# A hybrid streaming-encoder block on one core: longer warm-up, reordered first tiles and v normalisation, lag kernels in four partition groups, "down" by tokens with x1 added on TensorE

## The reference

```python
h = _rms(x, g_mix)
za, zu, zv, zq, zg = split(h @ w_in)          # 512, 512, 512, 512, 3*1024 columns
ya = gelu(_s5(za, ...))                       # diagonal state space, 32 groups of 16
ya = (ya * sigmoid(ya @ w_glu + b_glu)) @ w_a_out
yb = _sgu(zu, zv, g_sgu, beta_sgu, w_s, b_s) @ w_b_out
       # gelu(zu) * (causal mix over blocks of 128 tokens of layernorm(gelu(zv)) + b_s)
yc = _mem_xattn(zq, mem, g_mem, w_kv) @ w_c_out    # 4 heads of 128, softmax over 256
gates = sigmoid(zg + b_gate)
merged = gates[0] * ya + gates[1] * yb + gates[2] * yc
x = x + merged @ w_out                        # called x1 below
hf = _rms(x, g_ffn)
x = x + (silu(hf @ w_gate) * (hf @ w_up)) @ w_down   # x2; inner width 2816
return _rms(x, g_final)
```

## Time and profile before

| | us |
|---|---|
| median of 3 runs | 813.68 (812.5 to 813.94) |
| the profiled execution, its own time | 813.09 |
| its span, first to last instruction | 811.4 |
| PE busy | 790.8 (97%) |
| DVE busy | 413.4 (51%) |
| ACT busy | 356.6 (44%) |
| POOL busy | 354.1 (44%) |
| moved by DMA | 83.9 MB, 103 GB/s |

### The profile page before, as it was taken

How to read it: one execution, slowest core, us unless ns; L and a number is a source line. 1 busy time by engine, 2 the same in 40 slices (tenths; PEclk the granted TensorE clock), 3 DMA queues, 4 the chain that set the end, 5 groups by cost and what they waited for, 6 DMA issues and landing times.

```text
span 811.4 us, 10169 instructions
## 1 busy us (share of the span) xinstructions
PE 790.8 (97%) x3690; PEld 655.9 (81%) x3690; DVE 413.4 (51%) x625; ACT 356.6 (44%) x520; POOL 354.1 (44%) x182
## 2 busy tenths in 40 slices
PE   7999799999999999999999999999999999999996
PEld 6788687688888888888788788888888888888885
DVE  5899969856566665246765533333333333000035
ACT  5796355633535333634434444444433443122133
POOL 2556646234242434444344344444444444443452
PEclk8999899999999999999999999999999999999997
DMA  7743323022221343232323223322332233233313
GB/s 240 288 153 105 129 72 108 29 79 86 71 91 65 100 160 105 78 102 80 104 83 99 102 82 102 103 97 84 103 103 86 95 103 101 85 100 103 99 57 104
DMA packets 24814, 83.90 MB, mean 103 GB/s; under 512 B 2640, under 2 KB 4816, under 8 KB 24400
## 3 DMA queue, kind: packets, MB, share of 16 engines
q1 hardware_dynamic: 24784, 83.50, 31.0%
HBM read 81.39 MB, written 2.10 MB: 103 GB/s over the span
## 4 chain that ended last, share of the span: by engine, by line
PE 84%; DVE 9%; issue 3%; POOL 2%; DMA 1%; ACT 1%; SPq 0%; POOLq 0%; DVEq 0%; ACTq 0%
PE bank L1305 26%; PE bank L1307 26%; PE bank L1306 26%; DVE pow_tmp L803 2%; POOL w_lo L383 1%; PE bank L1514 1%; PE bank L1399 1%; PE bank L1524 1%; PE bank L1416 1%; DMA raw<-w_dram 1%; DVE vtok L969 1%; DVE mf L1175 1%; DVE bpow L803 1%; DVE tab_tmp L803 1%; DVE cpow L803 1%
## 5 line engine op out<-in xcount | busy, mean ns | idle before, releaser
L383 POOL TENSOR_TENSOR w_lo<-raw,w_hi 128x1024 fp32r<-128x1024 f32 x111 | 268.1, 2416 | 368.1 <-ACT w_hi L460 368.1
L460 ACT ACTIVATE w_hi<-raw 128x1024 fp32r<-128x1024 f32 x133 | 141.0, 1060 | 363.4 <-PE bank L1307 353.6
L1305 PE MATMUL bank<-h_hi,w_hi 128*128 128x512 f32 x640 | 252.6, 395 | 4.9 <-DVE h_lo L808 2.2
L1306 PE MATMUL bank<-h_lo,w_hi 128*128 128x512 f32 x640 | 250.3, 391 | 0.0
L1307 PE MATMUL bank<-h_hi,w_lo 128*128 128x512 f32 x640 | 250.2, 391 | 0.0
L1305 PEld LDWEIGHTS bank<-h_hi,w_hi 128*128 128x128 f32 x640 | 120.7, 189 | 32.7 <-issue 4.4
L1307 PEld LDWEIGHTS bank<-h_hi,w_lo 128*128 128x128 f32 x640 | 120.8, 189 | 25.4
L1306 PEld LDWEIGHTS bank<-h_lo,w_hi 128*128 128x128 f32 x640 | 120.7, 189 | 25.1 <-issue 0.5
L388 POOL TENSOR_TENSOR w_lo<-raw,w_hi 128x512 fp32r<-128x512 f32 x48 | 73.6, 1553 | 60.1 <-ACT w_hi L460 51.1
L1305 PE MATMUL bank<-act_hi,w_hi 128*128 (+2 forms) x176 | 67.0, 381 | 0.0
L1307 PE MATMUL bank<-act_hi,w_lo 128*128 (+2 forms) x176 | 66.8, 379 | 0.0
(11 more groups left out here) (248 smaller groups left out, 1128.9 us busy)
## 6 DMA issues: line engine op xcount, KB each, us to landing
raw<-w_dram SPq DMA_DIRECT2D x133, 512.0 KB, 3.4
xT<-xt_dram SPq DMA_DIRECT2D x6, 512.0 KB, 7.7
xtok<-xtok_dram SPq DMA_DIRECT2D x4, 512.0 KB, 6.6
out_dram<-xT SPq DMA_DIRECT2D x8, 256.0 KB, 2.2
raw<-w_dram SPq DMA_DIRECT2D x4, 256.0 KB, 6.9
xT<-xt_dram SPq DMA_DIRECT2D x4, 256.0 KB, 3.9
memf<-mem_dram SPq DMA_DIRECT2D x1, 1024.0 KB, 11.1
mtok<-mtok_dram SPq DMA_DIRECT2D x1, 1024.0 KB, 8.9
```

The costliest lines, as they stand in the source:

```text
L383: nc.gpsimd.tensor_tensor(w_lo[:, s, :], raw[:, s, :], fv(w_hi[:, s, :]), ALU.subtract).then_inc(w_ready, 1)
L460: nc.scalar.activation(w_hi[:, slot, :], raw[:, slot, :], ACT.Copy).then_inc(w_rounded, 1)
L1305: mm(out, a[0], b[0], start=first, stop=False)
L1306: mm(out, a[0], b[1], start=False, stop=False)
```

## The change

1. `WARM_UP` is 14, not 10.
2. The first two tiles: tile 1's sixth step comes after the end of tile 0, so tile 0 ends three products sooner.
3. `normalize_v(2)` and `(3)` go from before the last q to between later steps of DVE; the first table half goes ahead of `scale_u(1)`, the last table sum ahead of `scale_u(2)`, `head_scale(3)` ahead of `scale_u(3)`.
4. `kernels` puts each of the four blocks on 32 partitions of its own in bank 6 and runs the four blocks next to one another; DVE builds `toep` from the four groups with eight small operations.
5. w_out is written out, with eight banks. For each feature tile ACT also rounds x1 (two copies of 256 tokens) and DVE takes the rests (two subtractions).
6. `turn_x1` transposes x1 on PE by products with a rounded identity, hi and lo, 64 products of 128 moving columns, straight into the banks on which `down` then accumulates: 32 after the first hidden pair, 32 in `down`'s first tile.
7. `down` has 128 tokens stationary and 512 features of w_down moving; its loop is written out. A bank now holds 128 tokens by 512 features.
8. The last norm sums along columns: ACT's `Square` with a running sum, a root on ACT, a reciprocal and one scaling operation per bank on DVE, with g_final spread over partitions (`g_row`, loaded by DMA). POOL has no part in it. The stores go out by tokens.

```diff
-WARM_UP = 10
+WARM_UP = 14
@@ SP
+            sp.dma_start(g_row[:, :], row_d).then_inc(row_loaded, 16)
+            for t in range(4):
+                for n in range(2):
+                    if t == 3 and n == 1:
+                        sp.wait_ge(out_act, 1)
+                    else:
+                        sp.wait_ge(out_dve, 2 * t + n + 1)
+                    cols = slice(n * T, (n + 1) * T)
+                    sp.dma_start(out_d[t, :, cols], y_out[:, t, cols]).then_inc(out_stored, 16)
@@ ACT
+                nc.scalar.activation(x1b_hi[:, k, :], xT[:, k, HALF:T], ACT.Copy).then_inc(x1_hi_s, 1)
+                nc.scalar.activation(x1a_hi[:, k, :], xT[:, k, 0:HALF], ACT.Copy).then_inc(x1_hi_s, 1)
...
+            for t in range(4):
+                for n, ssq in enumerate((ssq0, ssq1)):
+                    act.wait_ge(dn_done, 2 * t + n + 1)
+                    if t:
+                        act.wait_ge(o_sq, 2 * t + n - 1)
+                    nc.scalar.activation(squares[:, n, :], bank[2 * t + n][:, :], ACT.Square,
+                                         accum_out=ssq[:, t:t + 1]).then_inc(o_sq, 1)
+                act.wait_ge(o_sq, 2 * t + 2)
+                act.wait_ge(o_bias, t + 1)
+                nc.scalar.activation(ostd[:, t:t + 1], ssq1[:, t:t + 1], ACT.Sqrt, bias=obias[:, t:t + 1],
+                                     scale=1.0 / D).then_inc(o_std, 1)
+            act.wait_ge(x2g_ready, 1)
+            act.wait_ge(o_rec, 4)
+            nc.scalar.activation(y_out[:, 3, T:D], x2g[:, :], ACT.Copy, scale=orec[:, 3:4]).then_inc(out_act, 1)
@@ DVE
             normalize_v(0)
+            take_qk(2)
             normalize_v(1)
-            normalize_v(2)
-            take_qk(2)
-            normalize_v(3)
             take_qk(3)
...
             scale_u(0)
+            normalize_v(2)
             take_pt(0)
             head_max(2)
+            table_half(NC // 2, (0,))
+            go(table_sum(NC // 2, 0))
             scale_u(1)
             head_scale(2)
-            table_half(NC // 2, (0,))
-            go(table_sum(NC // 2, 0))
             table_half(NC // 2, (1,))
+            table_sum(NC // 2, 1).then_inc(tables_ready, 1)
+            normalize_v(3)
             scale_u(2)
...
-            table_sum(NC // 2, 1).then_inc(tables_ready, 1)
+            head_scale(3)
             scale_u(3)
-            head_scale(3)
...
+                for q in range(ROUND):
+                    rows = slice(CH * q, CH * q + CH)
+                    go(V.tensor_copy(toep[0:CH, q, CH:P], bank[6][rows, CH:P]))
+                    go(V.scalar_tensor_tensor(toep[0:CH, q, 0:CH], ident[rows, rows], small[rows, C_D + 4 * m + q:C_D + 4 * m + q + 1],
+                                              bank[6][rows, 0:CH], ALU.mult, ALU.add))
...
+                dve.wait_ge(x1_hi_s, 2 * c + 1)
+                tt(x1b_lo[:, c, :], xT[:, c, HALF:T], fv(x1b_hi[:, c, :]), ALU.subtract).then_inc(x1_lo_s, 1)
+                dve.wait_ge(x1_hi_s, 2 * c + 2)
+                dve.wait_ge(x1_lo_s, 2 * c + 1)
+                tt(x1_low[:, c, HALF:T], xT[:, c, 0:HALF], fv(x1a_hi[:, c, :]), ALU.subtract).then_inc(x1_lo_s, 1)
...
+            for t in range(4):
+                dve.wait_ge(o_sq, 2 * t + 1)
+                V.tensor_scalar(obias[:, t:t + 1], ssq0[:, t:t + 1], 1.0 / D, EPS, ALU.mult, ALU.add).then_inc(o_bias, 1)
+                if t == 3:
+                    dve.wait_ge(o_sq, 8)
+                    tt(x2g[:, :], bank[7][:, :], g_row[:, T:D], ALU.mult).then_inc(x2g_ready, 1)
+                dve.wait_ge(o_std, t + 1)
+                V.reciprocal(orec[:, t:t + 1], ostd[:, t:t + 1]).then_inc(o_rec, 1)
+                dve.wait_ge(o_rec, t + 1)
+                for n in range(1 if t == 3 else 2):
+                    cols = slice(n * T, (n + 1) * T)
+                    V.scalar_tensor_tensor(y_out[:, t, cols], bank[2 * t + n][:, :], orec[:, t:t + 1], g_row[:, cols],
                                            ALU.mult, ALU.mult).then_inc(out_dve, 1)
@@ PE
+            for t, k0, k1 in ((0, 0, 2), (1, 0, 2), (0, 2, 4), (1, 2, 4), (0, 4, 6), (1, 4, 5), (0, 6, 8), (1, 5, 8)):
...
-                for q in range(ROUND):
-                    for i in range(2):
-                        ins = mm(bank[6][0:CH, q * P:(q + 1) * P], ba[i][:, q, L - 1, :],
+                for i in range(2):
+                    for q in range(ROUND):
+                        ins = mm(bank[6][CH * q:CH * q + CH, 0:P], ba[i][:, q, L - 1, :],
...
+            for c in range(KD):
+                if c == 0:
+                    pe.wait_ge(x1_ready, 4)
+                if c == 4:
+                    pe.wait_ge(j2_g, KD)
+                    pe.wait_ge(j2_prod, KD)
+                tile_ready(T_WO + c)
+                column_tile(bank[c][:, :], c % NS, merged if c == 0 else lambda k: pair(mg_hi, mg_lo, k), KD
+                            ).then_inc(w_used, 1)
...
+            def turn_x1(t):
+                rows = slice((t % 2) * P, (t % 2 + 1) * P)
+                low = slice(HALF + (t % 2) * P, HALF + (t % 2 + 1) * P)
+                for n in range(2):
+                    for j in range(4):
+                        k = 4 * n + j
+                        parts = (x1b_hi[:, k, rows], x1b_lo[:, k, rows]) if t >= 2 else (
+                            x1a_hi[:, k, rows], x1_low[:, k, low])
+                        for i, x in enumerate(parts):
+                            ins = mm(bank[2 * t + n][:, j * P:(j + 1) * P], x, ident_r[:, :],
+                                     start=j == 0 and i == 0, stop=False)
+                ins.then_inc(x1_turned, 1)
...
+            def down(hi, lo, w, t, n, last=False):
+                o = bank[2 * t + n][:, :]
+                cols, rows = slice(n * T, (n + 1) * T), slice(t * P, (t + 1) * P)
+                mm(o, hi[:, rows], w[0][:, cols], start=False, stop=False)
+                mm(o, hi[:, rows], w[1][:, cols], start=False, stop=False)
+                return mm(o, lo[:, rows], w[0][:, cols], start=False, stop=last)
...
+            for t in range(4):
+                for n in range(2):
+                    down(act_hi[:, KF - 2, :], act_lo[:, KF - 2, :], slot_weights(0), t, n)
+                    down(act_hi[:, KF - 1, :], act_lo[:, KF - 1, :], (last_hi, last_lo), t, n, True).then_inc(dn_done, 1)
```

More of the change, by code:

```diff
@@ L25 @@
 KF = FF // P
+HALF = T // 2
 HEADS = 4
@@ L74, with build @@
 SIN_MAX = 3.1415925
-def build(nc, xt_d, xtok_d, mem_d, mtok_d, small_d, sgu_d, w_d, out_d):
+def build(nc, xt_d, xtok_d, mem_d, mtok_d, small_d, sgu_d, row_d, w_d, out_d):
     F = mybir.dt.float32
@@ L1626, in _ @@
                 feed(i, 1, ff_u)
-            def down(slot, n, x, first, last):
-                return product(bank[n][:, :], weight(slot, 0, n * P, P, 0), x, first, last)
+            def down(hi, lo, w, t, n, last=False):
[4 more added lines that the diff above has]
+                return mm(o, lo[:, rows], w[0][:, cols], start=False, stop=last)
@@ L1632, in _, with slot_weights @@
+            def slot_weights(s):
+                return w_hi[:, s, :], w_lo[:, s, :]
             for k in range(2):
                 tile_ready(T_DN + k)
-                for n in (4, 5, 6, 7, 0, 1, 2, 3):
-                    if k == 0 and n == 0:
+                for t in (2, 3, 0, 1):
+                    if k == 0 and t == 0:
                         pe.wait_ge(ff_g, KF + 1)
                         pe.wait_ge(ff_u, KF + 1)
+                        turn_x1(0)
+                        turn_x1(1)
@@ L1650, in _ @@
-            for k in (KF - 4, KF - 3):
+            for k in range(2, KF - 2):
                 tile_ready(T_DN + k)
-                for n in range(KD):
-                    ins = down(k, n, pair(act_hi, act_lo, k), False, k == KF - 3)
-                    if k == KF - 3 and n < KD - 1:
-                        ins.then_inc(dn_part, 1)
+                for t in range(4):
+                    for n in range(2):
+                        ins = down(act_hi[:, k, :], act_lo[:, k, :], slot_weights(k % 2), t, n)
@@ L1666, in last_sum @@
-            def last_sum(h):
-                pe.wait_ge(sum_dve, 3 * h + 3)
-                pe.wait_ge(sum_pool, 2 * h + 2)
-                pe.wait_ge(x2_sq, KD * h + KD)
-                sums = (osum[:, 0, HALVES[h]], osum[:, 1, HALVES[h]], osq[:, KD - 1, HALVES[h]])
-                for t in range(HALF // P):
-                    for i, x in enumerate(sums):
-                        ins = mm(bank[0][:, t:t + 1], x[:, t * P:(t + 1) * P], ones[:, 0:1],
-                                 start=i == 0, stop=i == len(sums) - 1)
-                ins.then_inc(o_ssq, 1)
```

229 lines of the change are left out of this document (51 added, 178 removed).

## The result

| | us | range |
|---|---|---|
| before, 4 runs beside the next line | 813.81 | 812.5 to 814.93 |
| after, 4 runs | 800.52 | 799.57 to 802.63 |
| after again, 6 runs, later, beside before at 812.49 | 803.09 | 799.07 to 804.76 |

The ratio is 0.9842, 95% interval 0.9825 to 0.9859 (the second time 0.9871, 0.9847 to 0.9895). The ten runs of after together have a median of 801.7. Within its batch after is 13.3 us under before the first time and 9.4 the second. Forecast was 803.4, 798 to 811, a gain of 10.3. The profiled execution took 800.84 us (span 799.1), before 813.09 (811.4): 12.3 us for the forecast 10.3.

What follows compares the result with a forecast made beforehand. TensorE, busy 97% of the span, was taken as the bound. Terms 0.7 + 6.0 + 3.6 - 0.2 - 7.5 + 7.7 = 10.3 us off the median 813.68 gave 803.4 us, range 798 to 811.

Steps and rivals of the forecast that it cites:

- Start, +0.7: First tiles: tile 0's slot free 0.68 us earlier shortens PE's wait at tile 2; 0.7 us gained, nothing taken for the clock.
- v normalisation, +6.0: Last q to first gate: PE's 4.7 us wait and half clock go, DVE then bounds; 6.0 us gained, 5 to 7.3.
- Lag kernels, +3.6: Four lag-kernel rounds: four partition groups overlap, 0.9 us a round; 3.6 us gained, 0 to 5.6.
- two thirds of the possible: Lag kernels: of the 1.4 us a round that full overlap would give, 0.9 was taken.
- the upper bound of a factor of four (1.4): Lag kernels: four groups at a time, 1.87 / 4 = 0.47 us, would gain 1.4 us a round.
- w_out, -0.2: w_out tiles: DVE's two added subtractions lag 0.1 us a tile, seen at the first FFN tile's h_lo(7); 0.2 us lost.
- The rival of an 11 us avalanche: w_out: contended subtractions put DVE 1.4 us a tile behind, 11 us over eight, PE loses the clock; 816.5 us, chance 0.05.
- Turning, -7.5: Turning x1 on PE: 64 new products at 0.117 us each, priced like a lag-kernel record; 7.5 us lost.
- The dear case (0.234): Turning: each narrow fp32r product costs two records, 0.234 us; 7.5 us more, 810.9 us, chance 0.17.
- the cheap one (0.062): Turning: products at 0.062 us, 4.0 us in all; with full overlap, or a held clock, about 800, chance 0.10.
- End, +7.7: Last products and final norm: products end at 797.2, then 3.1 us of norm and 3.4 of stores; 7.7 us gained.
- "faster": Whole kernel: chance of being faster than before, put at 0.90; within 0.2% 0.05, slower 0.05.

Runs made afterwards that it cites:

- kernel 8: After with 16 warm-up steps, seven filler products before tile 1, v's second tile normalised behind vM's copies, last heads' four scalings on ScalarE: 798.87 us.
- kernel 9: kernel 8 with the first two tiles in the order of before: 798.92 us.
- kernel 2: After with the lag kernels' records back in one group of 32 partitions and DVE's three toep operations back: 805.33 us.
- kernels 3: Before with only the new start, v normalisation order and lag-kernel groups; w_out, turning and down as before: 804.14 us.
- kernel 4: After with two more DVE subtractions in each w_out tile, x1b_lo written three times over with the same values: 803.65 us, a single run.
- kernel 11: kernel 8 with the low half of x1 left out of the sum, 32 of 64 turning products: 795.43 us.
- kernel 5: After with ten warm-up steps in place of 14: 799.73 us.

## Why the prediction was right, point by point

- **Start, +0.7.** 0.4 at tile 2. In after "the next weights had about 1.4 us in hand" holds well enough (tile 3's first half was split at about 27.4, PE came to it at 28.6 without a wait). In kernel 8 it doesn't, and kernel 9 says that there the order is worth nothing at the end; whether the 0.4 reach the end in after wasn't tried. Clock: nothing was counted, and little came of it. The reading was short: "eight products" at half speed in before are about 14, and the six ahead of the second gap did get the whole clock in after. That gap, named in the prediction, grew by what they saved and more, and behind it the clock fell (whole up to 11.4, half to 14.8).
- **v normalisation, +6.0.** 5.8 at the first gate (6.2 less 0.4; by kernel 2's profile, with the same program up to there, it would be 7.3). The place and the reason fit: the last bias addition lies just ahead of the gate (147.46 to 148.15, gate at 148.20). But PE has no wait for it. The slack went in the 1.2 us for prob, which I had counted as gone with head_scale(3) moved up: the four scalings took 4.42 us beside GpSimd. DVE was the bound, and showed it one step earlier. By the beat of VectorE and GpSimd, which the prediction didn't have, this gain is also the one that varies: kernels 3 and 4, whose code up to the gate is that of after, reached it at 151.1.
- **Lag kernels, +3.6.** 5.2: 1.29 a round for 0.9. The guess of two thirds of the possible was too low; the upper bound of a factor of four (1.4) was nearly met. The small copies for toep, 0.22 to 0.26 us each, cost PE nothing.
- **w_out, -0.2.** 0. No DVE idle before x1, no PE wait; about 0.2 us between w_out and the end of down stay unplaced. The rival of an 11 us avalanche fell by kernel 4: I had let each late subtraction be contended and kept h_lo at 2.24, while being late took h_lo out of contention.
- **Turning, -7.5.** 7.04 = 64 x 0.11, and kernel 11 gives 0.11 by itself. Taking the fp32 record of equal width came out near, but by luck as far as is known: that record's 0.117 was no price of its width, since in four groups it took 0.036. The dear case (0.234) and the cheap one (0.062) both fell.
- **End, +7.7.** 8.2: the products 13.7 us to 11.1 and 0.3 for a w_lo (2.3 won for 2.8), and the tail 11.4 to 5.4 (5.9 won for 4.9). I had put one operation behind the other; x2g ran beside the root, and both halves of y_out side by side (794.41 and 795.2 in the rows above).

The sum of forecasts was 10.3, of measurements 0.4 + 5.8 + 5.2 + 0 - 7.0 + 8.2 - 0.2 = 12.4, against 12.3 of the spans. The miss of 2 us is the lag kernels' 1.6 and the end's 0.5; the others cancel. By the median of all ten runs of after the gain is 11 to 12 us (812.5 or 813.8, less 801.7), nearer to the forecast than the first four runs were. That is luck: the lag kernels and the end gave more than forecast, and five of the ten runs, at 802.6 to 804.8, gave some of it back in a way that the prediction didn't foresee; they have no trace. A small slip in the chances: by its own list "faster" is 0.92, not 0.90.

## What to carry to other kernels

Price a change where the last wait is, and ask what the freed engine owes next: three of the gains here (tile 2's weights in kernel 8, the early start, the moved scaling) were partly claimed by the next wait. Where executions differ by microseconds, compare a stretch between two landmarks of the trace rather than the whole time: nine profiles agreed within 0.5 us from the first gate on. Small products that fill one group of output partitions can be put in four groups, here at a third of the time. Turning an operand on TensorE is paid in full where TensorE never idles, and here took back 7.0 of the 8.2 us that a norm with tokens on partitions saves at the end.

## What was not expected of the hardware

- Four groups of 32 output partitions: 16 fp32 records, each with its own weight load, in 0.57 us for 1.86 in one group.
- fp32r products of 128 moving columns, 0.11 us apart: half the columns of a 256 one (0.117) for the same time.
- The beat of VectorE and GpSimd: eight 128x256 operations in 3.45 or 6.58 us, and 28.4 or 31.9 us for a whole chain, with a start 1 us earlier for the slower one.
- The granted clock at the start fell in some executions and held in others, for nearly the same instructions: in kernel 5 whole over pauses of 1.66 and 1.44 us, in after half behind pauses of 1.04 and 2.16. The four profiles in which it fell are also those whose warm-up products ran closest together.
